# Input x loaded in quarters with its own order of the first steps, four modulation sums moved, one weight unit rounded sooner, and a smaller GpSimd share of one unit

## The chip, the cores and the metric

The kernel runs on one core of one Trainium2 chip. The metric is device time in microseconds (us) of one launch; lower is better. The times of before are the median of three runs and one profiled execution.

## The reference: what is computed

Two blocks run one after the other on x, 256 tokens of 1024 channels, all in float32. The first block has two layers (neighborhood attention and differential attention side by side), the second two layers of a modulated stack (two feed-forward parts each, a pooling mixer or an attention between them). Cut to what matters here:

```python
def first_block(x, norm_g, w_in, ..., w_out, final_g):
    for l in range(2):
        h = rmsnorm(x, norm_g[l])
        proj = h @ w_in[l]                       # 1024 -> 4096 columns: q, k, v, gate, twice
        out_a = neighborhood_attention(q_a, k_a, v_a, na_rpb[l])
        out_b = diff_attention(q_b, k_b, v_b, t5_table, lam, lam_init, subln_g[l])
        y = concat([out_a * silu(g_a), out_b * silu(g_b)])
        x = x + y @ w_out[l]
    return rmsnorm(x, final_g)

def second_block(x, c, ada_w, ada_b, norm_g, ffn_w_in, ffn_w_out, ...):
    c_silu = silu(c)
    for layer in range(2):
        mods = split(c_silu @ ada_w[layer] + ada_b[layer], 9)     # 9 vectors of 1024
        sh, sc, g = mods[0], mods[1], mods[2]
        h = rms_norm(x, norm_g[layer, 0]) * (1 + sc) + sh
        x = x + 0.5 * (1 + g) * swiglu(h, ffn_w_in[layer, 0], ffn_w_out[layer, 0])
        ...                                       # pooling mixer (layer 0) or attention (layer 1)
        ...                                       # second feed-forward part
        if layer == 0: kv = shared_kv(x, c_silu, ...)             # 2 more such vectors
    return x
```

In all, 20 modulation vectors of 1024 numbers are matrix-vector products with `silu(c)`; they depend on nothing but the inputs.

## The kernel before, in words

**Weight units.** The weights are cut into 189 units of 128 partitions x 2048 columns (1 MB). Units 0 to 15 are the input projection of the first block's layer 0, 16 to 19 its output projection, 20 to 35 and 36 to 39 those of layer 1, 40 to 61 the first feed-forward part up, 62 to 72 down, 73 the pooling weights, 74 on the second feed-forward part, and so on. Each passes through four stations. SyncE's queue (SPq) loads it into `raw`, a ring of six. ScalarE (ACT) rounds it into `w_hi`, a ring of four (`fill` on ScalarE, L641). VectorE (DVE, `lows`, L1158), GpSimd (POOL, `low`, L510) or both in halves (`shared_units`: `low_first` on GpSimd, L521, and `low_second` on VectorE, L1168) write the rest, `w_lo`, in the place of `raw`. TensorE (PE) multiplies: each float32 product is three, `w_hi` by `h_hi` (L1822), `w_hi` by `h_lo` (L1827) and `w_lo` by `h_hi` (L1835), four matmuls of 512 columns each: twelve in one "half step", which is one unit for one of the two token tiles. Two half steps use up a unit.

**Activations.** A tile of x is turned by eight transposes of 128x128 (L1914), four for the first four channel blocks ("half 0") and four for the others ("half 1"), into job banks of PSUM, of which there are three in rotation. They are then split into `h_hi` and `h_lo`. For the first projection this is `first_norm` on ScalarE and on VectorE: raw x is turned, and the norm's factor is applied when the results leave PSUM. VectorE makes `h_hi` of half 0 (L1277) and all `h_lo` (L1269), ScalarE `h_hi` of half 1 (L805). The sum of squares (L812) comes later and must be there, with its root (L1292), before ScalarE takes group 0 out of PSUM (L844).

**Order of the first steps.** `first_steps` gives (group, tile, half): (0,0,0), (0,1,0) with unit 0, (0,0,1), (0,1,1) with unit 1, then group 1 with units 2 and 3. After step 6 TensorE turns group 0's result (L1960). x comes as two loads of 512 KB: tile 0 ahead of unit 0, tile 1 behind it. Unit 0 comes in two halves. A few matmuls on zeros (`warm_up`, L2022) fill the first microseconds.

**Modulation sums.** Each vector is made in two halves. VectorE accumulates eight scaled pieces (`ada`, L1137 and L1144) into `ada_acc`; then TensorE turns this sum with four transposes (`ada_sum`, L1849), and VectorE reduces it (`reduce_vector`, L1102) and, with the second half, adds and scales (L1108, L1115). `sum_step` says after which half step of a projection layer this happens, `sum_unit` after which unit elsewhere. They follow the accumulation's end (`half_end`), pushed out of quiet stretches.

**Order.** Every engine runs its list in program order and waits on semaphores; nothing is reordered by a planner. What stands behind a waiting instruction on an engine waits too.

Of the kernel before, what the change touches and what calls it, by code (L numbers as in the profile page):

```python
# [60 lines left out]
WARM_UP = (3, 1)  # L61
SUM_STEPS = (5, 7, 9, 11, 12, 14, 15, 18, 22, 29)
# [133 lines left out]
def program(nc, known, x_in, w_in, w_out, ffn_in, ffn_out, pool_w, w_kv, w_q, w_o, ada_w, kv_ada_w,  # L196
# [60 lines left out]
    with ExitStack() as ctx:  # L257
# [78 lines left out]
        x_in_sem = [ctx.enter_context(nc.semaphore(f"x_loaded{t}")) for t in range(NT)]  # L336
# [8 lines left out]
        first_in = ctx.enter_context(nc.semaphore("first_constants_loaded"))  # L345
# [4 lines left out]
        first_consts = [(ident[:], identity), (gcols[:], norm_cols)]  # L350
# [3 lines left out]
        N_FIRST, N_CONST = 16 * len(first_consts), 16 * len(consts)  # L354
# [27 lines left out]
        assert not pool_units & shared_units  # L382

# [64 lines left out]
        def _(sp):  # L448
            sp.dma_start(x[:, 0, :], x_in[0:P, :]).then_inc(x_in_sem[0], 16)
            for u in range(NU):  # L450
# [13 lines left out]
                if u == 0:  # L464
                    sp.dma_start(x[:, 1, :], x_in[P:2 * P, :]).then_inc(x_in_sem[1], 16)
# [29 lines left out]
        def _(pool):  # L495
# [19 lines left out]
            def low_first(u):  # L515

                if u in shared_units:
                    pool.wait_ge(*S.at("w_hi_ready", u) if u else S.at("first_hi_ready"))
                    for c in range(0, UNIT // 2, LOW_PIECE):
# [111 lines left out]
        def _(act):  # L631
# [59 lines left out]
            def norm(name, last, front=norm_front):  # L691
# [5 lines left out]
                if name == "a0":  # L697
                    act.wait_ge(first_in, N_FIRST)
# [47 lines left out]
            for into, src in first_consts:  # L746
                act.dma_start(into, src).then_inc(first_in, 16)
# [41 lines left out]
            def first_norm():  # L789
# [10 lines left out]
                act.wait_ge(first_in, N_FIRST)  # L800
                for t in range(NT):
                    act.wait_ge(*S.at("xT_done", "a0", t, 1))
# [287 lines left out]
        def _(dve):  # L1090
# [72 lines left out]
            def low_second(u):  # L1163

                if u in shared_units:
                    dve.wait_ge(*S.at("w_hi_ready", u))
                    piece = slice(UNIT // 2, UNIT)
# [5 lines left out]
            def sums(upto):  # L1173

                while sums_done[0] <= min(upto, NU - 1):
                    u = sums_done[0]
                    for v, half in HALVES:
                        e = sum_unit.get((v, half), NU)
                        if e + 4 == u and up_sum(e) is None:
                            reduce_vector(v, half)  # L1180
# [79 lines left out]
            def first_norm():  # L1260
# [24 lines left out]
                lows(2)  # L1285
# [155 lines left out]
            dve.wait_ge(first_in, N_FIRST)  # L1441
            for layer in range(DEPTH):
# [154 lines left out]
            modulate_half(1, 1)  # L1597
            pooled_low_half(1, 0)
# [174 lines left out]
        def _(pe):  # L1773
# [34 lines left out]
            def half_step(u, t, nk, k_in_lhs, lhs, banks, start, stop, done=None, between=lambda: None, lo_ready=()):  # L1808
# [9 lines left out]
                for k in range(nk):  # L1818
                    if u == 0 and k == nk // 2:
                        pe.wait_ge(*S.at("w_hi_ready", 0))  # L1820
                    for c, b in enumerate(banks):
                        pe.matmul(bank(b), hi[:, k_in_lhs + k, tok], wh[:, k, c * 512:(c + 1) * 512],  # L1822
                                  start=start and k == 0, stop=False)
                lhs_wait(lo_ready)
                for k in range(nk):
                    for c, b in enumerate(banks):
                        pe.matmul(bank(b), lo[:, k_in_lhs + k, tok], wh[:, k, c * 512:(c + 1) * 512],  # L1827
                                  start=False, stop=False)
# [88 lines left out]
            def norm_T(name, t, hat=None):  # L1917
                if name == "a0":
                    pe.wait_ge(x_in_sem[t], 16)
                for half in range(2):  # L1920
                    transpose_half(name, t, half, "xT_done", [("x_hat_ready", hat or name, t)] if name != "a0" else ())
# [215 lines left out]
            pool_product(0, acc_use((("pool",), 0), ("x_ready", "f01", 0)), (0, 1, 2, 3))  # L2137
            mix_across()
# [5 lines left out]
            ada_jobs(u)  # L2144
# [201 lines left out]
```

## Time and profile before

| | |
|---|---|
| runs (3) | median 1205.9 us, 1205.85 to 1205.99 |
| profiled execution | 1205.66 us, of which span 1203.8 us |
| busy: TensorE / VectorE / ScalarE / GpSimd | 1186.5 / 799.3 / 586.5 / 559.6 us |
| share of the span | 99% / 66% / 49% / 46% |
| TensorE clock granted | full throughout |
| HBM traffic | 297.92 MB, 247 GB/s over the span |

The span is what the profiler sees between the first and the last instruction. The groups of rows further down are of the timeline: start in us from the span's start, length in us, engine, line of the kernel, operation, tile written and tiles read, shape, and how many instructions the row merges. In brackets stands the idle time of that engine just before, and what ended it. Where a row merges several instructions, its length runs from the first start to the last end.

### The profile page before, as it was taken

Reading aid. Unit: us, or ns where it says so; the run is one execution under the profiler, and the core shown is the slowest. Engines: PE = TensorE matmul, PEld = TensorE weight load, DVE = VectorE, ACT = ScalarE, POOL = GpSimd, SP = SyncE. Lnnn points to the kernel's source line nnn. Section 1 sums busy time; section 2 is a strip of 40 time slices with the busy share of each in tenths; the row PEclk is TensorE's granted clock in tenths of the full one; section 3 lists DMA queues with packets and bytes.
Section 4 is the critical chain, followed back from the end, with each engine's and each line's share of the span. In section 5 each row is a group of like instructions: output and inputs, shape, how many; then the busy total and the mean of one; then the engine's idle time right before and its main releaser. Section 6 shows DMA issues by size and latency. Waiting matters only on the chain.

```text
span 1203.8 us, 15431 instructions
## 1 busy us (share of the span) xinstructions
PE 1186.5 (99%) x5752; PEld 975.2 (81%) x5752; DVE 799.3 (66%) x1118; ACT 586.5 (49%) x764; POOL 559.6 (46%) x418
## 2 busy tenths in 40 slices
PE   8999999999999999899999999999999999999998
PEld 6888888788788888788888888888888887888887
DVE  6885468845787687678768666697673675644423
ACT  5566465665643443454434357444352665534440
POOL 1465334564454443545445226764452464445360
PEclk9999999999999999999999999999999999999999
DMA  9976369845798899459888748798884444766650
GB/s 349 356 273 234 105 237 334 280 163 172 243 342 289 293 343 352 159 164 337 296 311 312 276 175 276 248 330 299 308 295 166 150 154 157 262 215 204 210 192 35
DMA packets 183224, 297.92 MB, mean 247 GB/s; under 512 B 8368, under 2 KB 100208, under 8 KB 183152
## 3 DMA queue, kind: packets, MB, share of 16 engines
q1 hardware_dynamic: 177696, 284.82, 68.4%
q10 hardware_dynamic: 5456, 12.13, 3.0%
q8 instruction: 46, 0.75, 0.3%
q14 instruction: 26, 0.21, 0.1%
HBM read 295.84 MB, written 1.08 MB: 247 GB/s over the span
## 4 chain that ended last, share of the span: by engine, by line
PE 88%; DVE 5%; ACT 2%; POOL 2%; issue 1%; SPq 1%; DMA 1%; ACTq 0%; DVEq 0%
PE ps L1822 26%; PE ps L1835 26%; PE ps L1827 26%; PE ps L2088 2%; PE ps L1849 1%; PE ps L1972 1%; PE ps L1914 1%; PE ps L2000 1%; PE ps L1988 1%; POOL stat L501 1%; DMA raw<-w_in 1%; DVE w_lo L1158 1%; ACT w_hi L641 1%; PE ps L1960 1%; PE ps L2011 1%
## 5 line engine op out<-in xcount | busy, mean ns | idle before, releaser
L510 POOL TENSOR_TENSOR w_lo<-raw,w_hi 128x512 fp32r<-128x512 f32 x348 | 478.6, 1407 | 447.8 <-ACT w_hi L641 447.8
L641 ACT ACTIVATE w_hi<-raw 128x2048 fp32r<-128x2048 f32 x188 | 354.4, 1909 | 103.1 <-PE ps L1835 68.3
L1822 PE MATMUL ps<-w_hi,h_hi 128*128 128x512 f32 x1120 | 313.6, 402 | 1.4 <-issue 0.8
L1835 PE MATMUL ps<-w_lo,h_hi 128*128 128x512 f32 x1120 | 301.4, 391 | 1.4 <-POOL w_lo L510 0.5
L1827 PE MATMUL ps<-w_hi,h_lo 128*128 128x512 f32 x1120 | 300.5, 390 | 0.0
L1158 DVE TENSOR_TENSOR w_lo<-raw,w_hi 128x2048 fp32r<-128x2048 f32 x96 | 224.5, 2342 | 111.8 <-ACT w_hi L641 108.1
L1835 PEld LDWEIGHTS ps<-w_lo,h_hi 128*128 128x128 f32 x1120 | 209.3, 188 | 48.8 <-DVE w_lo L1158 1.7
L1827 PEld LDWEIGHTS ps<-w_hi,h_lo 128*128 128x128 f32 x1120 | 210.2, 188 | 46.0 <-DVE h_lo L1219 0.2
L1822 PEld LDWEIGHTS ps<-w_hi,h_hi 128*128 128x128 f32 x1120 | 200.6, 188 | 44.0 <-issue 6.8
L1144 DVE SCALAR_TENSOR_TENSOR ps<-ada_raw,ccol,ps 128x512 f32<-128x512 f32 x240 | 181.1, 754 | 9.1 <-DMA ada_raw<-ada_w 2.4
L914 ACT ACTIVATE a_hi<-ps 128x512 fp32r<-128x512 f32 x44 | 26.3, 599 | 160.8 <-PE ps L2088 160.8
L501 POOL TENSOR_TENSOR stat<-stat,minus_half 128x1 f32<-128x1 f32 (+3 forms) x25 | 29.1, 1166 | 151.1 <-DVE stat L1195 115.6
L1822 PE MATMUL ps<-w_hi,a_hi 128*128 128x512 f32 x348 | 95.7, 397 | 0.0
L1835 PE MATMUL ps<-w_lo,a_hi 128*128 128x512 f32 x348 | 93.8, 391 | 0.0
L1827 PE MATMUL ps<-w_hi,a_lo 128*128 128x512 f32 x348 | 93.7, 391 | 0.0
L1835 PEld LDWEIGHTS ps<-w_lo,a_hi 128*128 128x128 f32 x348 | 65.3, 188 | 14.5
L1827 PEld LDWEIGHTS ps<-w_hi,a_lo 128*128 128x128 f32 x348 | 65.4, 188 | 14.3
L1822 PEld LDWEIGHTS ps<-w_hi,a_hi 128*128 128x128 f32 x348 | 64.0, 188 | 12.9
L924 ACT ACTIVATE hn<-ps 128x512 f32<-128x512 f32 x44 | 26.3, 598 | 93.8 <-PE ps L1835 93.8
L1510 DVE SCALAR_TENSOR_TENSOR hn<-hn,ps 128x512 f32<-128x512 f32 x44 | 30.2, 686 | 58.7 <-ACT hn L924 58.6
L1503 DVE TENSOR_TENSOR a_lo<-ps,a_hi 128x512 fp32r<-128x512 f32 x44 | 30.4, 691 | 41.6 <-ACT a_hi L914 40.6
L735 ACT ACTIVATE pr<-lg,stat 128x256 f32<-128x256 f32 x64 | 31.9, 500 | 53.1 <-DVE stat L1303 53.1
(198 smaller groups left out, 979.7 us busy)
## 6 DMA issues: line engine op xcount, KB each, us to landing
raw<-ffn_in SPq DMA_DIRECT2D x176, 512.0 KB, 5.8
ada_raw<-ada_w SPq DMA_DIRECT2D x144, 512.0 KB, 7.3
raw<-ffn_out SPq DMA_DIRECT2D x44, 1024.0 KB, 6.7
raw<-w_in SPq DMA_DIRECT2D x31, 1024.0 KB, 8.5
raw<-w_out SPq DMA_DIRECT2D x8, 1024.0 KB, 6.2
ada_raw<-kv_ada_w SPq DMA_DIRECT2D x16, 512.0 KB, 9.0
raw<-w_kv SPq DMA_DIRECT2D x8, 1024.0 KB, 5.6
bias<-na_bias ACTq DMA_DIRECT2D x16, 256.0 KB, 4.3
```

Of the source, the lines that this page charges most:

```text
L501: pool.tensor_tensor(st(at, n), st(at, n), minus_half[:, 0:n], ALU.pow).then_inc(*S.inc("rsqrt_ready", *key))
L510: ins = pool.tensor_tensor(w_lo[:, u % RAW, piece], raw[:, u % RAW, piece], w_hi[:, u % RING, piece].bitcast(F32), ALU.subtract)
L641: act.activation(w_hi[:, u % RING, :], raw[:, u % RAW, :], ACT.Copy).then_inc(*S.inc("w_hi_ready", u))
L735: ins = act.activation(pr1[:, w, t, :], lg1[:, s, t, :], ACT.Exp, bias=st(rs + 2 + t), scale=-1.0, accum_out=st(rs + t))
L914: act.activation(a_hi[:, 2 * g:2 * g + 2, :].rearrange("p k c -> p (k c)"), bank(b), ACT.Copy).then_inc(*S.inc("a_hi_ready", name, g))
L1144: ins = dve.scalar_tensor_tensor(out=into, in0=src, scalar=c, in1=acc, op0=ALU.mult, op1=ALU.add)
L1158: dve.tensor_tensor(w_lo[:, u % RAW, :], raw[:, u % RAW, :], w_hi[:, u % RING, :].bitcast(F32), ALU.subtract).then_inc(*S.inc("w_lo_dve", u))
L1503: dve.tensor_tensor(a_lo[sl].rearrange("p k c -> p (k c)"), bank(b), a_hi[sl].rearrange("p k c -> p (k c)").bitcast(F32), ALU.subtract).th ...
L1510: link(dve.scalar_tensor_tensor(out=ffn_gate, in0=ffn_tanh, scalar=1.0, in1=ps[:, b:b + 2, 0:GC], op0=ALU.add, op1=ALU.mult))
L1822: pe.matmul(bank(b), hi[:, k_in_lhs + k, tok], wh[:, k, c * 512:(c + 1) * 512], start=start and k == 0, stop=False)
L1827: pe.matmul(bank(b), lo[:, k_in_lhs + k, tok], wh[:, k, c * 512:(c + 1) * 512], start=False, stop=False)
L1835: ins = pe.matmul(bank(b), hi[:, k_in_lhs + k, tok], wl[:, k, c * 512:(c + 1) * 512], start=False, stop=stop and k == nk - 1)
```

## The change

1. **x in quarters.** x comes as four loads of 256 KB (`load_x(t, half)`), the quarter (tile 0, half 0) ahead of unit 0, the other three behind it, each with a semaphore. The identity and the norm's columns have a semaphore each: the transposes wait for the identity alone.
2. **Order of the first steps.** TensorE turns one quarter before step 0, one inside step 0 and the two quarters of half 1 inside step 1, each time ahead of the `w_lo` matmuls. Steps 0 and 1 use the first half of unit 0 with both `h_hi` and `h_lo` before its second half. On ScalarE unit 1 is rounded between the two tiles' `h_hi` of half 1; `w_lo` of unit 1 stands between their `h_lo` on VectorE. `WARM_UP` goes from (3, 1) to (2, 1).
3. **Four moved sums.** In both projection layers the sum after step 29 goes to after step 31, and its reduction to behind the four `h_hi`/`h_lo` steps that follow on VectorE. Another goes from unit 43 to unit 45. The last one ahead of the pooling weights goes from unit 68 to unit 73 (`in_pool`), between the first pooling product and the mixing products of the second tile.
4. **A unit sooner.** ScalarE rounds unit `o + 4` (unit 20 in layer 0) behind the output projection's `h_hi`, ahead of the next norm's squares. In layer 1 this unit stood there already.
5. **GpSimd's share.** `shared_at`: of unit 158 GpSimd takes the first 512 columns and VectorE 1536, where each took 1024.

```diff
-WARM_UP = (3, 1)
-SUM_STEPS = (5, 7, 9, 11, 12, 14, 15, 18, 22, 29)
+WARM_UP = (2, 1)
+SUM_STEPS = (5, 7, 9, 11, 12, 14, 15, 18, 22, 31)
...
-        for a, b, wait in ((*QUIET[0], 3), (*QUIET[1], 1), (("up", 0, 0), ("up", 0, 0), 3)):
+        for a, b, wait in ((*QUIET[0], 3), (*QUIET[1], 1), (("up", 0, 0), ("up", 0, 0), 5)):
...
+    in_pool = max(h for h in sum_unit if sum_unit[h] < first["pool"])
+    sum_unit[in_pool] = first["pool"]
...
+        def shared_at(u):
+            return LOW_PIECE if u == first["up", 1, 1] + 2 else UNIT // 2
...
         @block.sync
-            sp.dma_start(x[:, 0, :], x_in[0:P, :]).then_inc(x_in_sem[0], 16)
+            def load_x(t, half):
+                cols = slice(512 * half, 512 * half + 512)
+                sp.dma_start(x[:, t, cols], x_in[t * P:(t + 1) * P, cols]).then_inc(x_in_sem[t][half], 16)
+            load_x(0, 0)
...
                 if u == 0:
-                    sp.dma_start(x[:, 1, :], x_in[P:2 * P, :]).then_inc(x_in_sem[1], 16)
+                    for t, half in ((1, 0), (0, 1), (1, 1)):
+                        load_x(t, half)
...
         first_norm() on ScalarE
-                act.wait_ge(first_in, N_FIRST)
+                act.wait_ge(gcols_in, 16)
                 for t in range(NT):
+                    if t:
+                        fill(1)
                     act.wait_ge(*S.at("xT_done", "a0", t, 1))
...
-                fill(1)
+                fill(2)
                 act.wait_ge(*S.at("stat_filled"))
                 for t in range(NT):
-                    act.wait_ge(x_in_sem[t], 16)
+                    for half in range(2):
+                        act.wait_ge(x_in_sem[t][half], 16)
                     act.activation(hn[:, t, :], x[:, t, :], ACT.Square, accum_out=st(t)).then_inc(
                         *S.inc("squares_ready", "a0", t))
-                    fill(2 + t)
-                fill(4)
+                    fill(3 + t)
...
         end of a projection layer on ScalarE, inside the loop over layers
                     high_part(("y", layer), t, 0, "yT_done")
-
-            fill(first["up", 0, 0])
+                fill(o + 4)
...
         first_norm() on VectorE
                 for t in range(NT):
                     first_low(t, 1)
-                lows(2)
+                    lows(1 + t)
...
         end of a projection layer on VectorE
                     low_part(("y", layer), t, 0, "yT_done")
+                for half in sum_step.get((layer, 31), []):
+                    reduce_vector(*half)
                 fill(o + 3)
...
             modulate_half(1, 1)
+            reduce_vector(*in_pool)
             pooled_low_half(1, 0)
...
         half_step() on TensorE
-                for k in range(nk):
-                    if u == 0 and k == nk // 2:
+                for part in (range(0, nk // 2), range(nk // 2, nk)) if u == 0 else (range(nk),):
+                    if u == 0 and part[0]:
                         pe.wait_ge(*S.at("w_hi_ready", 0))
...              (w_hi by h_hi, then lhs_wait(lo_ready), then w_hi by h_lo, for the k of each part)
                 def between(s):
                     if s == 0 and not layer:
-                        norm_T(name, 1)
+                        raw_T(1, 0)
+                    if s == 1 and not layer:
+                        raw_T(0, 1)
+                        raw_T(1, 1)
...
             pool_product(0, acc_use((("pool",), 0), ("x_ready", "f01", 0)), (0, 1, 2, 3))
+            ada_jobs(u)
             mix_across()
```

What stands in a row on TensorE at the start of the program, before (`ps<-ident,x` are the transposes of x, `ps<-row` the matmuls on zeros):

```order
L2022 MATMUL ps<-row 128x512 x3
L1914 MATMUL ps<-ident,x 128x128 x8
L2022 MATMUL ps<-row 128x512
L1822 MATMUL ps<-w_hi,h_hi 128x512 x4
L1827 MATMUL ps<-w_hi,h_lo 128x512 x4
L1914 MATMUL ps<-ident,x 128x128 x8
L1835 MATMUL ps<-w_lo,h_hi 128x512 x4
L1822 MATMUL ps<-w_hi,h_hi 128x512 x4
L1827 MATMUL ps<-w_hi,h_lo 128x512 x4
L1835 MATMUL ps<-w_lo,h_hi 128x512 x4
```

And now, from the second transposes on (lines 1839, 1844, 1852 and 1931 are 1822, 1827, 1835 and 1914 of before):

```order
L1839 MATMUL ps<-w_hi,h_hi 128x512 x2
L1844 MATMUL ps<-w_hi,h_lo 128x512 x2
L1931 MATMUL ps<-ident,x 128x128 x4
L1852 MATMUL ps<-w_lo,h_hi 128x512 x4
L1839 MATMUL ps<-w_hi,h_hi 128x512 x2
L1844 MATMUL ps<-w_hi,h_lo 128x512 x2
L1839 MATMUL ps<-w_hi,h_hi 128x512 x2
L1844 MATMUL ps<-w_hi,h_lo 128x512 x2
L1931 MATMUL ps<-ident,x 128x128 x8
L1852 MATMUL ps<-w_lo,h_hi 128x512 x4
```

All sixteen transposes stood ahead of the first `w_lo` matmuls; now eight of them, those of half 1, stand behind step 1's `w_hi` matmuls.

ScalarE from the first rounding on, before (`w_hi<-raw` of 1024 columns is a half of unit 0, of 2048 columns units 1, 2, 3 and 4 in turn; `hn,stat<-x` are the squares of one tile):

```order
L797 ACTIVATE w_hi<-raw 128x1024
L805 ACTIVATE h_hi<-ps,gcols 128x128 x8
L641 ACTIVATE w_hi<-raw 128x2048
L812 ACTIVATE hn,stat<-x 128x1024
L641 ACTIVATE w_hi<-raw 128x2048
L812 ACTIVATE hn,stat<-x 128x1024
L641 ACTIVATE w_hi<-raw 128x2048 x2
```

And now:

```order
L808 ACTIVATE w_hi<-raw 128x1024
L818 ACTIVATE h_hi<-ps,gcols 128x128 x4
L652 ACTIVATE w_hi<-raw 128x2048
L818 ACTIVATE h_hi<-ps,gcols 128x128 x4
L652 ACTIVATE w_hi<-raw 128x2048
L826 ACTIVATE hn,stat<-x 128x1024
L652 ACTIVATE w_hi<-raw 128x2048
L826 ACTIVATE hn,stat<-x 128x1024
L652 ACTIVATE w_hi<-raw 128x2048
```

The rounding of unit 1 stands behind `h_hi` of (tile 0, half 1), which waits for the moved transposes; unit 2 now stands ahead of the first squares, unit 3 between them.

VectorE at the end of layer 0's projection, before (`mods<-` is the reduced sum, `w_lo<-raw,w_hi` x2 are units 18 and 19):

```order
L1219 TENSOR_TENSOR yn_lo<-ps,yn_hi 128x4x128
L1102 TENSOR_REDUCE mods<-ps 128x4
L1108 TENSOR_TENSOR mods<-mods,bcols 128x8
L1115 SCALAR_TENSOR_TENSOR mods<-mods,gcols 128x8
L1458 SCALAR_TENSOR_TENSOR ga<-ga,ps 128x1024
...
L1207 TENSOR_TENSOR ps<-ps,subc 128x512
L1219 TENSOR_TENSOR h_lo<-ps,h_hi 128x4x128
L1158 TENSOR_TENSOR w_lo<-raw,w_hi 128x2048 x2
```

And now:

```order
L1232 TENSOR_TENSOR yn_lo<-ps,yn_hi 128x4x128
L1471 SCALAR_TENSOR_TENSOR ga<-ga,ps 128x1024
...
L1220 TENSOR_TENSOR ps<-ps,subc 128x512
L1232 TENSOR_TENSOR h_lo<-ps,h_hi 128x4x128
L1115 TENSOR_REDUCE mods<-ps 128x4
L1121 TENSOR_TENSOR mods<-mods,bcols 128x8
L1128 SCALAR_TENSOR_TENSOR mods<-mods,gcols 128x8
L1171 TENSOR_TENSOR w_lo<-raw,w_hi 128x2048 x2
```

The three operations of the sum stand directly ahead of `w_lo` of unit 18. In layer 1 it is the reduction alone, ahead of unit 38.

## Rows read from the trace of the kernel before

**Rows 1.** The page, part 1: busy time of TensorE, share, instructions.
```profile
PE 1186.5 (99%) x5752; PEld 975.2 (81%) x5752; DVE 799.3 (66%) x1118; ACT 586.5 (49%) x764; POOL 559.6 (46%) x418
```

**Rows 2.** Timeline of the first 31 us, the instructions that set the start.
```profile
6.65 1.09 PE L1914 MATMUL ps<-ident,x 128*128 128x128 f32 x8 [0.85 <-DMA gcols<-norm_cols]
7.11 1.06 ACT L794 ACTIVATE w_hi<-raw 128x1024 fp32r<-128x1024 f32 x1 [3.95 <-DMA raw<-w_in]
...
8.32 3.61 POOL L521 TENSOR_TENSOR w_lo<-raw,w_hi 128x512 fp32r<-128x512 f32 x2 [7.48 <-ACT w_hi L794]
8.47 1.06 ACT L797 ACTIVATE w_hi<-raw 128x1024 fp32r<-128x1024 f32 x1 [0.30 <-DMA raw<-w_in]
...
9.56 1.23 DVE L1168 TENSOR_TENSOR w_lo<-raw,w_hi 128x1024 fp32r<-128x1024 f32 x1 [0.29 <-ACT w_hi L797]
...
11.98 1.20 PE L1835 MATMUL ps<-w_lo,h_hi 128*128 128x512 f32 x4
12.15 1.14 ACT L805 ACTIVATE h_hi<-ps,gcols 128x128 fp32r<-128x128 f32 x4 [1.59 <-PE ps L1914]
...
13.16 1.93 ACT L641 ACTIVATE w_hi<-raw 128x2048 fp32r<-128x2048 f32 x1
...
14.97 1.07 ACT L812 ACTIVATE hn<-x 128x1024 f32<-128x1024 f32 x1
...
15.75 1.07 PE L1822 MATMUL ps<-w_hi,h_hi 128*128 128x512 f32 x4
...
22.39 1.92 ACT L641 ACTIVATE w_hi<-raw 128x2048 fp32r<-128x2048 f32 x1 [1.61 <-DMA raw<-w_in]
...
26.55 0.16 DVE L1292 TENSOR_SCALAR stat<-stat 128x2 f32<-128x2 f32 x1
...
28.70 1.26 ACT L844 ACTIVATE hn<-ps,stat 128x512 f32<-128x512 f32 x2 [0.72 <-issue]
...
30.02 1.09 PE L1960 MATMUL ps<-ident,hn 128*128 128x128 f32 x8
```

**Rows 3.** Timeline of the ends of both projection layers.
```profile
121.75 0.60 PE L1849 MATMUL ps<-ident,ada_acc 128*128 128x128 f32 x4
...
124.35 0.68 DVE L1102 TENSOR_REDUCE mods<-ps 128x4 f32<-128x512 f32 x1
...
125.26 0.17 DVE L1115 SCALAR_TENSOR_TENSOR mods<-mods,gcols 128x8 f32<-128x8 f32 x1
...
131.49 1.16 PE L1822 MATMUL ps<-w_hi,yn_hi 128*128 128x512 f32 x4 [0.56 <-DVE ga L1458]
...
140.67 4.48 DVE L1158 TENSOR_TENSOR w_lo<-raw,w_hi 128x2048 fp32r<-128x2048 f32 x2
...
143.10 1.11 PE L1835 MATMUL ps<-w_lo,h_hi 128*128 128x512 f32 x4
...
278.21 1.16 PE L1822 MATMUL ps<-w_hi,yn_hi 128*128 128x512 f32 x4 [0.24 <-DVE ga L1458]
```

**Rows 4.** Timeline where layer 1's projection begins (unit 20).
```profile
153.26 5.05 POOL L510 TENSOR_TENSOR w_lo<-raw,w_hi 128x512 fp32r<-128x512 f32 x4 [3.06 <-ACT w_hi L641]
...
158.37 1.19 PE L1835 MATMUL ps<-w_lo,h_hi 128*128 128x512 f32 x4 [0.54 <-POOL w_lo L510]
```

**Rows 5.** Timeline, the sum after unit 43.
```profile
328.94 0.66 PE L1849 MATMUL ps<-ident,ada_acc 128*128 128x128 f32 x4 [0.72 <-DVE ada_acc L1144]
```

**Rows 6.** Timeline of the pooling mixer, second tile.
```profile
507.29 1.13 PE L1927 MATMUL ps<-bands,hn 128*128 128x128 f32 x8 [2.27 <-DVE hn L1570]
...
509.98 0.69 DVE L1581 TENSOR_TENSOR h_lo<-ps,h_hi 128x512 fp32r<-128x512 f32 x1 [1.38 <-ACT h_hi L955]
```

**Rows 7.** Timeline where the last feed-forward part begins (units 157 and 158).
```profile
1015.80 1.67 DVE L1168 TENSOR_TENSOR w_lo<-raw,w_hi 128x1024 fp32r<-128x1024 f32 x1
...
1018.67 1.20 PE L1835 MATMUL ps<-w_lo,h_hi 128*128 128x512 f32 x4 [0.47 <-POOL w_lo L521]
...
1020.37 1.09 PE L1914 MATMUL ps<-ident,hn 128*128 128x128 f32 x8 [0.51 <-ACT hn L654]
```

More of the change, by code:

```diff
@@ L335, in program @@
         bias_in = [ctx.enter_context(nc.semaphore(f"bias_in{i}")) for i in range(BIASES)]
-        x_in_sem = [ctx.enter_context(nc.semaphore(f"x_loaded{t}")) for t in range(NT)]
+        x_in_sem = [[ctx.enter_context(nc.semaphore(f"x_loaded{t}_{half}")) for half in range(2)] for t in range(NT)]
         ROWS = {("down", 0, 0): 2, "pool": 5, "pool_scale": 4, "pool_shift": 3, ("down", 0, 1): 8,
@@ L344, in program @@
         half_in = ctx.enter_context(nc.semaphore("first_half_loaded"))
-        first_in = ctx.enter_context(nc.semaphore("first_constants_loaded"))
+        ident_in = ctx.enter_context(nc.semaphore("identity_loaded"))
+        gcols_in = ctx.enter_context(nc.semaphore("norm_columns_loaded"))
         const_in = ctx.enter_context(nc.semaphore("constants_loaded"))
@@ L349, in program @@
         out_sem = ctx.enter_context(nc.semaphore("out_stored"))
-        first_consts = [(ident[:], identity), (gcols[:], norm_cols)]
         consts = [(bcols[:], ada_b_cols),
@@ L518, in low_first @@
                     pool.wait_ge(*S.at("w_hi_ready", u) if u else S.at("first_hi_ready"))
-                    for c in range(0, UNIT // 2, LOW_PIECE):
+                    for c in range(0, shared_at(u), LOW_PIECE):
                         piece = slice(c, c + LOW_PIECE)
@@ L744, in load_bias @@
                     bias_in[i % BIASES], 16)
-            for into, src in first_consts:
-                act.dma_start(into, src).then_inc(first_in, 16)
+            act.dma_start(ident[:], identity).then_inc(ident_in, 16)
+            act.dma_start(gcols[:], norm_cols).then_inc(gcols_in, 16)
             act.wait_ge(*S.at("minus_half_ready"))
@@ L1166, in low_second @@
                     dve.wait_ge(*S.at("w_hi_ready", u))
-                    piece = slice(UNIT // 2, UNIT)
+                    piece = slice(shared_at(u), UNIT)
                     dve.tensor_tensor(w_lo[:, u % RAW, piece], raw[:, u % RAW, piece],
@@ L1178, in sums @@
                         e = sum_unit.get((v, half), NU)
-                        if e + 4 == u and up_sum(e) is None:
+                        if e + 4 == u and up_sum(e) is None and e != first["pool"]:
                             reduce_vector(v, half)
@@ L1440, in _ @@
             dve.memset(stat[:], 1.0).then_inc(*S.inc("stat_filled"))
-            dve.wait_ge(first_in, N_FIRST)
+            dve.wait_ge(gcols_in, 16)
             for layer in range(DEPTH):
@@ L1817, in half_step @@
                     return
-                for k in range(nk):
-                    if u == 0 and k == nk // 2:
+                for part in (range(0, nk // 2), range(nk // 2, nk)) if u == 0 else (range(nk),):
+                    if u == 0 and part[0]:
                         pe.wait_ge(*S.at("w_hi_ready", 0))
[L1821 to L1828, printed above, removed]
+                    for k in part:
+                        for c, b in enumerate(banks):
+                            pe.matmul(bank(b), hi[:, k_in_lhs + k, tok], wh[:, k, c * 512:(c + 1) * 512],
+                                      start=start and k == 0, stop=False)
+                    lhs_wait(lo_ready)
+                    for k in part:
+                        for c, b in enumerate(banks):
+                            pe.matmul(bank(b), lo[:, k_in_lhs + k, tok], wh[:, k, c * 512:(c + 1) * 512],
+                                      start=False, stop=False)
                 between()
@@ L1917, in norm_T, with raw_T @@
             def norm_T(name, t, hat=None):
-                if name == "a0":
-                    pe.wait_ge(x_in_sem[t], 16)
                 for half in range(2):
-                    transpose_half(name, t, half, "xT_done", [("x_hat_ready", hat or name, t)] if name != "a0" else ())
+                    transpose_half(name, t, half, "xT_done", [("x_hat_ready", hat or name, t)])
+            def raw_T(t, half):
+                pe.wait_ge(x_in_sem[t][half], 16)
+                transpose_half("a0", t, half, "xT_done")
             def mix_part(half, to, of):
@@ L2025, in _ @@
             warm_up(WARM_UP[0])
-            pe.wait_ge(first_in, N_FIRST)
+            pe.wait_ge(ident_in, 16)
             for layer in range(DEPTH):
@@ L2029, in _ @@
                 if layer == 0:
-                    norm_T(name, 0)
+                    raw_T(0, 0)
                     warm_up(WARM_UP[1])
@@ L2143, in _ @@
             S.same("unit_used", (u,), "acc_done", (("pool",), NT - 1))
-            ada_jobs(u)
             ffn(0, 1, "f01", 8, "kv")
```

4 lines of the change are left out of this document (2 added, 2 removed).

## Prediction

> **What bounds the kernel now.** I read the page first: TensorE is busy for 1186.5 us of a span of 1203.8 us [rows 1]. So this kernel can only win what is left of TensorE's idle time, some 17 us, and it loses whatever makes TensorE wait more. Then I listed TensorE's own rows of the timeline that carry a bracket, since each is a wait that the other engines did not cover, and looked at the two or three engines around each: the start, the ends of the two projection layers, the first units after a norm, the pooling mixer. Each edit sits at one of these places. Between them TensorE runs without a gap, so a delay at one place moves all behind it and is not made good; every engine hangs from TensorE's step ends there. The sum is therefore a sum of shifts.
>
> **The start: what it removes.** TensorE waits for the norm's columns at 6.65 before its first transposes [rows 2]; now it waits for the identity alone. That gives nothing by itself: the next matmuls wait for ScalarE's rounding of the first half of unit 0. This half was there at 7.11 and the second at 8.47, so 512 KB take 1.36 us of the queue. With a quarter of x less ahead (256 KB) both come 0.68 us sooner, at about 6.43 and 7.79; at worst, no sooner. GpSimd's two pieces of `w_lo`, 3.61 us long, followed the first rounding at once and TensorE's first `w_lo` matmuls came at 11.98, right at the end of these pieces (8.32 + 3.61 = 11.93) [rows 2]. Now: rounding done 7.5, pieces done 11.3, `w_lo` matmuls at 11.3. The gain here is 0.68 us. The third warm-up matmul and the finer order of steps 0 and 1 lie inside this wait and cost nothing. The two more load commands delay the commands behind them; the cover is unit 4, which came at 22.39 with ScalarE waiting for it [rows 2], and which ScalarE reaches now only at 24.8 (below).
>
> **The start: what it adds.** A half step without waits takes at most (30.02 - 15.75)/5 = 2.85 us, and 2.73 when the waits in it are taken off; four matmuls are a third, 0.91. After 11.3: four `w_lo` matmuls 0.91, step 1's eight `w_hi` matmuls 1.82, four transposes of the quarter (0,1) 0.55 (the four of [rows 3] at 121.75 take 0.60 with their tail). ScalarE gets them at 14.6. It has been idle since 8.9, because what is queued next is `h_hi` of this quarter, and the rounding of unit 1 is queued behind that. So `h_hi` 1.14, to 15.8; rounding of unit 1 1.93, to 17.7 [durations, rows 2]. Step 2 needs both and starts at 17.8, where it started at 15.75 before: 2.05 us later. Before, unit 1 was rounded at 13.16 to 15.09, since the transposes stood ahead of the first `w_lo` matmuls.
>
> The loss grows behind it. ScalarE goes on: `h_hi` of (1,1) 1.14, unit 2 1.93, squares 1.04, unit 3 1.93, squares 1.04: 17.7 + 7.1 = 24.8. VectorE waits for the second squares before it takes `w_lo` of units 3 and 4 (2.24 us each, 4.48 for two [rows 3]), and only then makes the root's half (L1292): 25.0 + 4.6 = 29.7, where it was 26.55. ScalarE's evacuation of group 0 followed 2.15 us behind (28.70) and TensorE's L1960 3.47 us behind (30.02) [rows 2]. So L1960 comes at 33.2, 3.2 us late. TensorE itself would be there at 17.8 + 5 x 2.73 + 0.5 (a wait for `w_lo` of unit 1, which VectorE has at 17.8 + 2.3 = 20.1 against 19.6) = 31.9; it waits 1.3. From there on everybody is shifted alike. **Start: +3.2 us**, and 2.4 to 4.3 if each of these steps is a little shorter, or if the halves come no sooner.
>
> **The ends of the projection layers.** The four transposes of the sum (an `L1849` row; 0.44 us of TensorE's stream, from 121.75 to the next matmuls without their tail) leave the stream before the wait for the gate and go into it. This wait is 0.56 us in layer 0 and 0.24 us in layer 1 [rows 3]; in layer 1 what is over moves the next chain, which hangs from the same step end. I take -0.44 each, 0 to -0.56. But the reduction now stands directly ahead of `w_lo` of unit 18 on VectorE. That ran 140.67 to 142.96, and TensorE's `w_lo` matmuls began at 143.10: no slack, beyond 0.1. In layer 0 the three operations took 124.35 to 125.43, 1.08 us, so TensorE stalls 1.0; in layer 1 it is the reduction alone, 0.68, and the same pattern, so 0.65. Bounds: 0 (if VectorE got to it earlier) to 1.1 and 0.7. Both ends together: -0.9 + 1.65 = **+0.75**.
>
> **Unit 20 sooner.** GpSimd's four pieces began at 153.26 after waiting 3.06 us for ScalarE, which had the norm's squares and scaling ahead of the rounding, and TensorE waited 0.54 for them [rows 4]. ScalarE has the time for the rounding while it waits for x. **-0.54**, 0 at the other end.
>
> **Unit 43 to 45.** The wait of 0.72 for VectorE's accumulation goes [rows 5]; two units later the sum is long done. **-0.72**.
>
> **Unit 68 to 73.** The transposes leave a full stretch and go ahead of the mixing products, where TensorE waits 2.27 us for VectorE [rows 6]. The whole chain that ends this wait begins at a step end behind unit 68, so it comes 0.44 sooner: **-0.44**. The reduction (0.68) is put on VectorE ahead of `h_lo` at 509.98, ahead of which it idled 1.38 waiting for ScalarE [rows 6]; that covers it. Without this cover it would cost up to 0.68.
>
> **Unit 158.** TensorE waited 0.47 for GpSimd's pieces and then 0.51 for the scaled x [rows 7]. VectorE's part grows from 1024 to 1536 columns: 1.23 us alone [rows 2] becomes 1.8, and here 1024 took 1.67, so about 2.2, from 1015.80 to 1018.0. The first wait goes, but the mean for the norm's root is queued behind this operation, so the second wait grows by most of it: **-0.2**, between -0.47 and +0.1.
>
> The Trainium skill bears on this place: "SBUF — State Buffer", section "Who interferes with whom", says that a VectorE operation with two SBUF inputs and a GpSimd one that reads SBUF exclude each other for the whole instruction, whoever is first. The trace agrees in that 1.67 against 1.23 is a delay, not a rate; by the rule VectorE's operation would end at 1018.1, and the sum would be the same.
>
> **Sum.** +3.2 + 0.75 - 0.54 - 0.72 - 0.44 - 0.2 = +2.05 us. The profiled execution took 1205.66 us; the changed one 1207.7. The median of the runs is 0.24 above the profiled one: **1208.0 us**. About 0.2% (2.4 us: 1203.5 to 1208.3) is what a measurement of this kernel can tell from no change, so this is just inside.
>
> **Rivals.**
> - *The start gives its 0.68 us and takes nothing back.* This needs ScalarE to have `h_hi` of (0,1) and unit 1 rounded by 15.1, as before. For it: the start's edits all shorten the first wait. Against it: ScalarE's list, in which unit 1 stands behind the moved transposes. Sum -0.68 + 0.75 - 1.9 = -1.8, 1204.1; with the stalls of unit 18 and 38 hidden as well, -3.5, 1202.4.
> - *Slower: the halves of unit 0 come no sooner.* Place: the first rounding at 7.11. The three loads share the engines, so a smaller load ahead need not bring those behind it forward. Price: the 0.68 comes back on the whole chain, as all of it hangs from GpSimd's pieces: +2.7, 1208.6. It decides from a first rounding later than about 6.8: then the sum passes 2.4.
> - *The port.* GpSimd's second piece and VectorE's half of unit 0 become ready together, at about 8.9. Before, VectorE's 1.23 us came first (its operation at 9.56 kept its length, while GpSimd's pair took 3.61 us). If GpSimd's piece is first, the `w_lo` matmuls are no later, but VectorE's `h_hi` of (1,0) is, and with it step 1: 0.4 to 0.7 later, 1208.5. The rule of the Trainium skill named above (section "Who interferes with whom") allows this order, since by it whoever starts first keeps the port.
>
> **How the numbers follow.** Forecast 0.45, start without loss 0.2, halves no sooner 0.22, the port 0.13. The forecast's own range is 1206.3 to 1209.6: start 2.4 to 4.3, the encoder's stalls half to full, the other gains each 70 to 100%. The range to hold 8 in 10 reaches on to the first rival: 1204.0 to 1209.9. Faster: half of the first rival and a rest of unknown slack, 0.13. Slower: most of the second and third and the upper third of the forecast, 0.4. Same: 0.47.
>
> **What would show it.** Right: ScalarE idle for 5 us or more between the second half of unit 0 and `h_hi` of (0,1); the third group of `w_hi` matmuls (step 2) at 17 to 18.5 with TensorE waiting for ScalarE; a wait of about 1 us before the first `ps<-ident,hn` transposes, at about 33; waits of 1.0 and 0.65 us for `w_lo` of units 18 and 38; no wait at unit 20, none for `ada_acc` after unit 45; the wait in the mixer 0.4 to 0.5 shorter. Wrong: a step 2 that starts before 16.5, or `w_lo` of unit 18 in time although the sum stands ahead of it.

## The result, and the profile after

The changed kernel takes 1207.2 us by median (20 runs, 1206.1 to 1209.3), the kernel before 1205.9 in the same comparison (20 runs, 1205.0 to 1206.5). The ratio is 1.0013, with a 95% interval of 1.0007 to 1.0018: slower by 0.8 to 2.2 us, which is inside the 0.2% named in the prediction. The forecast was 1208.0. Ten of the 20 runs of after had a mean granted TensorE clock of 1.000 and a median of 1206.7; the ten others, with 0.997 to 0.999, took 1207.2 to 1209.3.

The profiled execution of after took 1206.67 us, its span 1204.7. The page's first part answers to [rows 1]: TensorE is busy for 0.9 us more, VectorE for 2.9 us more. Of this, 1.4 us is its halves of the units shared with GpSimd (9.2 for 7.8): its larger share of unit 158, and a wait for GpSimd inside its operation for unit 0 (below). The rest is spread over small operations.

```profile
PE 1187.4 (99%) x5750; PEld 976.4 (81%) x5750; DVE 802.2 (67%) x1118; ACT 585.9 (49%) x764; POOL 560.6 (47%) x417
```

Timeline of the start of after, against [rows 2]. Columns as there: start and length in us, engine, line, what is written and read, and in brackets the idle time before it with what ended it.

```profile
5.50 1.06 ACT L805 ACTIVATE w_hi<-raw 128x1024 fp32r<-128x1024 f32 x1 [2.33 <-DMA raw<-w_in]
...
6.70 2.52 POOL L532 TENSOR_TENSOR w_lo<-raw,w_hi 128x512 fp32r<-128x512 f32 x2 [5.86 <-ACT w_hi L805]
...
8.20 2.12 DVE L1181 TENSOR_TENSOR w_lo<-raw,w_hi 128x1024 fp32r<-128x1024 f32 x1
...
10.46 1.17 PE L1852 MATMUL ps<-w_lo,h_hi 128*128 128x512 f32 x4 [0.26 <-DVE w_lo L1181]
...
14.34 1.14 ACT L818 ACTIVATE h_hi<-ps,gcols 128x128 fp32r<-128x128 f32 x4 [6.18 <-PE ps L1931]
15.35 1.93 ACT L652 ACTIVATE w_hi<-raw 128x2048 fp32r<-128x2048 f32 x1
...
17.42 1.16 PE L1839 MATMUL ps<-w_hi,h_hi 128*128 128x512 f32 x4 [1.83 <-ACT w_hi L652]
...
32.06 1.09 PE L1979 MATMUL ps<-ident,hn 128*128 128x128 f32 x8 [0.28 <-ACT hn L857]
```

The first `w_lo` matmuls come 1.52 us sooner than before (10.46 against 11.98). Then ScalarE stands idle for 6.18 us, with unit 1's rounding queued behind the transposes of the quarter (0,1). TensorE waits 1.83 us for that rounding, and the transposes of the turned result come at 32.06, 2.04 us later than in [rows 2].

Behind the start, rows of after against [rows 3 to 7]:

```profile
142.38 0.68 DVE L1115 TENSOR_REDUCE mods<-ps 128x4 f32<-128x512 f32 x1
...
143.50 4.49 DVE L1171 TENSOR_TENSOR w_lo<-raw,w_hi 128x2048 fp32r<-128x2048 f32 x2
...
145.84 1.20 PE L1852 MATMUL ps<-w_lo,h_hi 128*128 128x512 f32 x4 [0.88 <-DVE w_lo L1171]
...
163.87 4.50 DVE L1171 TENSOR_TENSOR w_lo<-raw,w_hi 128x2048 fp32r<-128x2048 f32 x2 [0.67 <-POOL stat L512]
...
166.22 1.21 PE L1852 MATMUL ps<-w_lo,h_hi 128*128 128x512 f32 x4
...
292.47 1.19 PE L1852 MATMUL ps<-w_lo,h_hi 128*128 128x512 f32 x4 [0.35 <-DVE w_lo L1171]
...
508.60 1.13 PE L1946 MATMUL ps<-bands,hn 128*128 128x128 f32 x8 [1.84 <-DVE hn L1585]
...
1017.10 2.21 DVE L1181 TENSOR_TENSOR w_lo<-raw,w_hi 128x1536 fp32r<-128x1536 f32 x1
```

The waits at the gates (131.49 and 278.21 before), at unit 20 (158.37), behind unit 43 (328.94) and for GpSimd at unit 158 (1018.67) are gone. New are 0.88 and 0.35 us for `w_lo` behind the moved sums: VectorE begins with the reduction at 142.38 and comes to `w_lo` only at 143.50. The mixer's wait is 1.84 instead of 2.27. One more place is new, with no bracket because the idle time is short: at 166.22, behind unit 20, `w_lo` comes 0.4 us late for TensorE (told below with the sum).

### The profile page after: what moved, and what is told of

It reads as the page before. It is cut to its first block, busy times and chain, and to the rows that moved or that the text cites. A ratio compares the mean times of both kernels' runs of the same rounds, so it can differ in the third digit from the quotient of the medians.

```text
span 1204.7 us, 15430 instructions
## 1 busy us (share of the span) xinstructions
PE 1187.4 (99%) x5750; PEld 976.4 (81%) x5750; DVE 802.2 (67%) x1118; ACT 585.9 (49%) x764; POOL 560.6 (47%) x417
## 4 chain that ended last, share of the span: by engine, by line
PE 88%; DVE 6%; ACT 3%; issue 2%; POOL 1%; DMA 0%; SPq 0%; ACTq 0%; DVEq 0%
PE ps L1839 26%; PE ps L1852 26%; PE ps L1844 26%; PE ps L2110 2%; PE ps L1931 1%; PE ps L1991 1%; PE ps L1866 1%; DVE w_lo L1171 1%; PE ps L2019 1%; PE ps L2007 1%; ACT w_hi L652 1%; POOL stat L512 1%; PE ps L1979 1%; PE ps L2030 1%; ACT h_hi L672 1%
## 5 line engine op out<-in xcount | busy, mean ns | idle before, releaser
L1518 DVE TENSOR_TENSOR a_lo<-ps,a_hi 128x512 fp32r<-128x512 f32 x44 | 30.4, 692 | 40.7 <-ACT a_hi L927 39.7
```

The lines of the kernel that those rows point to most:

```text
L1518: dve.tensor_tensor(a_lo[sl].rearrange("p k c -> p (k c)"), bank(b), a_hi[sl].rearrange("p k c -> p (k c)").bitcast(F32), ALU.subtract).th ...
```

## The experiments

Ratios are to the kernel before, timed in the same comparison. Experiments 1 to 4, 5 to 8, and 9 and 10 are three such comparisons; the kernel before had 1205.6, 1205.9 and 1205.6 us in them, and the changed kernel was in none, so its 1207.2 is that of the result.

**1. The start alone** (the kernel before with the start's edits: quarters, order, semaphores, `WARM_UP = (2, 1)`).

> The kernel before with the start's edits alone (x in quarters, the order of the first steps, two warm-up matmuls ahead); sums, unit 20 and unit 158 as before. Theory (the start costs, the rest gives back): in the changed kernel the first transposes of the turned result stood at 32.06 against 30.02, so 2.0 us later than before, 1207.9 us by median, and more where the clock rises late. Rival (the start is free, the rest costs): within 0.3 of before, 1206.0.

1208.9 us (6 runs), ratio 1.0028 (1.0016 to 1.0039): 3.3 us slower. The start costs more than the whole change, and the theory held in sign; the size is larger than the 2.0 that the trace of after shows. Why is told below, with the landings.

**2. The rest alone** (before's start; sums, unit 20, unit 158 as changed).

> The changed kernel's moved sums, unit 20 and unit 158 with the start of before. Theory: the shifts behind the start in the changed kernel's trace go from +2.04 to +0.90, so this is 1.1 us faster than before, 1204.8 by median, with stalls of 0.9 and 0.35 us for w_lo of units 18 and 38, and with a spread of runs as narrow as before (1.6 us). Rival (the rest costs, by my sum's terms with the stalls at 1.0 and 0.65 and the gains not there): 1206.5.

1203.7 us, ratio 0.9984 (0.9975 to 0.9993): 1.9 us faster, range 1203.4 to 1204.3. The two parts add up: +3.3 - 1.9 = +1.4, and the change as a whole measured +1.3. The waits of 0.88 and 0.35 us stand in this trace too, at 142.68 (the row below) and 289.31:

```profile
142.68 1.20 PE L1844 MATMUL ps<-w_lo,h_hi 128*128 128x512 f32 x4 [0.88 <-DVE w_lo L1164]
```

**3. The third warm-up matmul back.**

```diff
-WARM_UP = (2, 1)
+WARM_UP = (3, 1)
```

> The changed kernel with the third warm-up matmul back. Theory A (the clock): the third matmul fills TensorE until the identity comes; with it the engine gets its full clock at about 4.5 us as before, and the runs of 1207.3 to 1209.3 with a mean granted clock below 1 go: median 1206.6, spread under 1.5 us. Theory B (my prediction: the third matmul lies in a wait and costs nothing): same times as the changed kernel, 1207.2, with the same spread of 3 us.

1208.5 us, ratio 1.0025 (1.0015 to 1.0035): 1.2 us slower than the changed kernel. Both theories fell; full clock came at 7.49 us in this trace, not at 4.5 as the first had it. TensorE's rows of this kernel:

```profile
1.45 5.49 PE L2041 MATMUL ps<-row 128*128 128x512 f32 x6 [1.45 <-DVE row L1452]
6.73 0.98 PE L1931 MATMUL ps<-ident,x 128*128 128x128 f32 x4
7.54 1.02 PE L2041 MATMUL ps<-row 128*128 128x512 f32 x2
8.57 0.74 PE L1839 MATMUL ps<-w_hi,h_hi 128*128 128x512 f32 x2
```

The transposes wait for nothing but the warm-up, which runs to 6.73; in after they stood at 5.03. The first `w_hi` matmuls come at 8.57 instead of 6.95, the first `w_lo` matmuls at 11.57 instead of 10.46. The turned result comes at 33.68, so between these two traces the third matmul costs 1.6 to 1.7 us.

**4. Unit 1 ahead of `h_hi` of (0,1) on ScalarE.**

```diff
+                fill(1)
                 for t in range(NT):
-                    if t:
-                        fill(1)
```

> The changed kernel with one line of ScalarE's list moved: unit 1 is rounded ahead of h_hi of (0,1) instead of behind it. Theory (ScalarE's list sets the start): step 2 begins at 15.6 to 16.2 instead of 17.42, the first transposes of the turned result at 30.4 to 30.8 instead of 32.06, and the time falls by 1.2 to 1.6 us. Rival (unit 1 itself comes late, or the squares chain sets 32.06 by itself): step 2 after 17, time as the changed kernel.

1206.2 us, ratio 1.0005 (0.9996 to 1.0014): 1.0 us less than the changed kernel, where 1.2 to 1.6 were expected. The rows:

```profile
12.52 1.92 ACT L652 ACTIVATE w_hi<-raw 128x2048 fp32r<-128x2048 f32 x1 [3.69 <-DMA raw<-w_in]
...
14.59 2.17 ACT L817 ACTIVATE h_hi<-ps,gcols 128x128 fp32r<-128x128 f32 x8
...
15.76 1.13 DVE L1281 SCALAR_TENSOR_TENSOR h_lo<-ps,gcols,h_hi 128x128 fp32r<-128x128 f32 x4 [3.35 <-ACT h_hi L817]
15.78 1.19 PE L1838 MATMUL ps<-w_hi,h_hi 128*128 128x512 f32 x4
...
16.80 2.28 DVE L1170 TENSOR_TENSOR w_lo<-raw,w_hi 128x2048 fp32r<-128x2048 f32 x1
...
19.14 1.20 PE L1851 MATMUL ps<-w_lo,h_hi 128*128 128x512 f32 x4 [1.00 <-DVE w_lo L1170]
```

Step 2 begins at 15.78 without a wait, as expected. But 1.00 us of the gain is lost at 19.14, where TensorE waits for `w_lo` of unit 1: VectorE has `h_lo` of (0,1), which still hangs from the late transposes, ahead of it. The turned result comes at 31.07, where 30.4 to 30.8 was expected.

**5. The transposes of (0,1) ahead of the first `w_lo` matmuls.**

```diff
                     if s == 0 and not layer:
                         raw_T(1, 0)
+                        raw_T(0, 1)
                     if s == 1 and not layer:
-                        raw_T(0, 1)
                         raw_T(1, 1)
```

> The changed kernel with the transposes of the quarter (0,1) ahead of the first w_lo matmuls instead of behind step 1's w_lo wait. Theory (the place of these transposes in TensorE's order holds up ScalarE): h_hi of (0,1) at about 11 instead of 14.34, unit 1 rounded when it lands (12.5), step 2 at about 16 without a wait, the first transposes of the turned result at 29.8 to 30.5 instead of 32.06, time 1.6 to 2.2 us less, 1205.3. Rival (only ScalarE's order matters): no better than unit 1 first, 31.1 and 1206.2.

1205.3 us, ratio 0.9995 (0.9987 to 1.0004): 1.9 us less than the changed kernel. The rows:

```profile
9.51 1.03 PE L1931 MATMUL ps<-ident,x 128*128 128x128 f32 x8
...
10.64 1.15 ACT L818 ACTIVATE h_hi<-ps,gcols 128x128 fp32r<-128x128 f32 x4 [2.22 <-PE ps L1931]
...
12.28 1.92 ACT L652 ACTIVATE w_hi<-raw 128x2048 fp32r<-128x2048 f32 x1 [0.49 <-DMA raw<-w_in]
...
14.92 1.08 PE L1839 MATMUL ps<-w_hi,h_hi 128*128 128x512 f32 x4
...
29.86 1.09 PE L1979 MATMUL ps<-ident,hn 128*128 128x128 f32 x8 [1.15 <-ACT hn L857]
```

ScalarE has `h_hi` of (0,1) at 10.64 and rounds unit 1 at 12.28, when it lands; step 2 begins at 14.92 without a wait, and the turned result comes at 29.86, now behind a wait of 1.15 us for ScalarE. So the place of these four transposes in TensorE's order causes 1.9 of the start's 3.3 us; ScalarE's list is how it gets to the other engines. The full clock came early in this trace (4.47 us, 6.92 in after), but that isn't what made the difference: in experiment 10, which has these transposes in the same place, it came at 6.29, and step 2 began at 15.01.

**6. The sums of step 31 reduced behind the output projection's `w_lo`.**

```diff
-                for half in sum_step.get((layer, 31), []):
-                    reduce_vector(*half)
                 fill(o + 3)
+                for half in sum_step.get((layer, 31), []):
+                    reduce_vector(*half)
```

> The changed kernel with the reduction of the step-31 sums moved on VectorE from ahead of w_lo of units 18 to 19 (38 to 39) to behind it. Theory (the reduction is what makes TensorE wait): the waits of 0.88 and 0.35 us for w_lo at 145.84 and 292.47 go, the hole before the output projection stays closed, and the time falls by 1.2 to 1.5 us, to about 1205.9. Rival (ScalarE's rounding of the unit is late anyway, since it too runs into the layer's end): the waits stay above 0.5 in sum and the time falls by less than 0.5.

1205.8 us, ratio 0.9998 (0.9989 to 1.0007): 1.4 us less than the changed kernel. VectorE and TensorE there:

```profile
142.40 4.48 DVE L1171 TENSOR_TENSOR w_lo<-raw,w_hi 128x2048 fp32r<-128x2048 f32 x2
...
144.83 1.11 PE L1852 MATMUL ps<-w_lo,h_hi 128*128 128x512 f32 x4
...
146.80 0.69 DVE L1115 TENSOR_REDUCE mods<-ps 128x4 f32<-128x512 f32 x1
...
148.77 1.23 DVE L1269 TENSOR_TENSOR x<-ps,x 128x1024 f32<-128x1024 f32 x1 [0.88 <-PE ps L1852]
```

`w_lo` begins at 142.40 instead of 143.50 and TensorE doesn't wait. The reduction now lies in VectorE's idle time ahead of the update of x, of which 0.88 us is still left.

**7. The same with the start of before** (experiments 2 and 6 together).

> The start of before, all other edits of the change, and the reduction of the step-31 sums behind w_lo of units 18/19 and 38/39. If the three effects add: 1203.7 - 1.2 = 1202.5 us, 3 us faster than before. Rival (the parts overlap: what is gained at the layer's end is lost in the next norm, whose transposes need a bank or whose x update needs VectorE): 1203.5.

1202.6 us, ratio 0.9972 (0.9962 to 0.9983). The effects add; this is 3.3 us faster than before and, across comparisons, 4.7 faster than the changed kernel.

**8. Two warm-up matmuls in the kernel before.**

```diff
-WARM_UP = (3, 1)
+WARM_UP = (2, 1)
```

> The kernel before with two warm-up matmuls ahead of the transposes instead of three. Theory (in the start of before the transposes wait for the norm's columns, so the third warm-up matmul costs nothing there; it costs 1.2 us only where the transposes wait for the identity alone): no change, within 0.4 us of before, transposes still after 5.8. Rival (it costs in any start): 1 us faster. Third possibility (it is needed for the clock): full clock later and 0.5 us or more slower.

1207.0 us, ratio 1.0009 (1.0000 to 1.0018): some 1.1 us slower (0 to 2.2), where I expected no change. The start doesn't show it (the turned result comes at 29.12). The profiled execution has a stretch at the lower clock right behind the mixer's wait. By stretch: from and to, us, busy time of TensorE, its weight loads, VectorE, ScalarE and GpSimd, then the granted clock:

```profile
505.00:507.00 2.00, 0.53 (x5) 0.56 (x6) 1.97 (x4) 1.12 (x2) 0.53 (x1) 1.00 0.00 1
507.00:508.00 1.00, 0.81 (x7) 0.58 (x6) 0.74 (x2) 0.51 (x1) 1.00 (x2) 0.72 0.00 0
508.00:510.00 2.00, 2.00 (x10) 2.00 (x11) 0.69 (x1) 1.18 (x3) 2.00 (x2) 0.50 0.00 0
```

Up to the mixer TensorE is 0.9 us ahead of the trace of before, and behind this stretch 0.1 us late: it cost 1.0 us in this execution. All 11 of its runs had a mean granted clock below 1.000. But so had 27 of the 29 runs of before in this comparison, and those took 1205.9 and not 1207. What makes this kernel slower stays open.

**9. Experiments 5 and 6 together.**

> The changed kernel with both mends: the transposes of the quarter (0,1) ahead of the first w_lo matmuls, and the step-31 reductions behind the output projection's w_lo. If they add (1.9 and 1.4 us off the changed kernel's 1207.2): 1204.0. Its start still ends in a wait of 1.15 us of TensorE for ScalarE's evacuation of group 0 (at 29.86), so it stays 1.4 us behind the start of before with the same mended sums, 1202.6.

1203.2 us, ratio 0.9981 (0.9972 to 0.9990): a little better than the sum. The wait for ScalarE ahead of the turned result is there, 0.86 us in this trace, the slowest of the 11 runs: the second half of unit 0 was rounded only at 9.09.

**10. The same, with VectorE's `w_lo` of unit 4 behind the root's half and the small constants.**

```diff
-                lows(4)
+                lows(3)
                 dve.wait_ge(*S.at("rsqrt_ready", "a0"))
                 dve.tensor_scalar(st(2, NT), st(0, NT), 0.5, ...).then_inc(*S.inc("half_root_ready"))
...
                     constants()
+                    lows(4)
```

> The kernel of the run e_T_early_late with VectorE's w_lo of unit 4 moved behind the norm's root half and the small constants. Theory (my prediction's step: VectorE takes w_lo of units 3 and 4 ahead of what the evacuation waits for, and this sets the first transposes of the turned result): ScalarE's evacuation goes ahead at 26.5 instead of 28.54, the wait of 1.15 us goes, 28.7 instead of 29.86, time 1202.9. Rival (w_lo of unit 4 then comes late, or the constants wait for their loads): the wait moves to another place and the time stays at 1204.0.

1202.6 us, ratio 0.9975 (0.9966 to 0.9984), 0.6 less than experiment 9, where 1.1 was expected. The small constants and the evacuation come at once:

```profile
24.17 0.17 DVE L1305 TENSOR_SCALAR stat<-stat 128x2 f32<-128x2 f32 x1 [0.60 <-POOL stat L512]
24.25 0.61 DVE L1325 TENSOR_TENSOR lamr<-lamr 128x128 f32<-128x128 f32 x2
...
26.33 1.27 ACT L857 ACTIVATE hn<-ps,stat 128x512 f32<-128x512 f32 x2 [0.72 <-PE ps L1853]
...
27.30 2.29 DVE L1171 TENSOR_TENSOR w_lo<-raw,w_hi 128x2048 fp32r<-128x2048 f32 x1
...
28.67 1.03 PE L1980 MATMUL ps<-ident,hn 128*128 128x128 f32 x8
```

The theory held in its mechanism: the wait is gone, and `w_lo` of unit 4 is in time at 27.30. The gain is half of what was expected. This kernel (new start, mended twice) and that of experiment 7 (old start) both beat the kernel before, by 3.0 and 3.3 us: mended, the new start draws level with the old one and is no gain over it. No run has x in quarters with the old order of steps, so what the four loads do by themselves isn't shown.

## Why the prediction was right, step by step

The forecast was 0.8 us above the measured median, and +2.05 us on the profiled time where the profiled executions differ by 1.0. Between these two traces all of this gap lies in the start, +2.04 for +3.2. By the runs of experiments 1 and 2 it lies in the rest: -1.9 for -1.15, and the start is +3.3. That the start's size fits the runs so well is partly luck: my end point, 33.2, was 1.1 us too late, and the 30.02 that I counted from was 0.9 us later than in three other traces of the old start.

*Start, predicted +3.2.* In the two profiled executions it is 30.02 to 32.06, +2.04; alone, by runs, it is +3.3. The difference is mostly what the profile of before happened to show. In it the first half of unit 0 was rounded at 7.11 [rows 2]. In the traces of three more kernels with this start it was 6.05, 6.04 and 6.18, and the turned result came at 29.00, 29.18 and 29.12: the execution that I had read was 1 us late there. The eight traces with x in quarters have 5.19 to 5.67. So 256 KB less ahead is worth 0.67 us (mean 5.42 against 6.09), where I took 0.68; against the one trace that I had it looks like 1.61. And with the new order the turned result goes from 29.1 to 32.06, 3.0 us later.

*How the loss comes about.* The mechanism was as told: ScalarE idle for over 5 us (6.18), step 2 at 17.4 (predicted 17.8), waiting for the rounding of unit 1. What sets the first `w_lo` matmuls was wrong. I had them at 11.3, at the end of GpSimd's pieces; these ended at 9.22, and the matmuls came at 10.46, waiting 0.26 us for VectorE's half. The last link was too long. I had the turned result at 33.2 with a wait of 1.3 us, and it came at 32.06 with 0.28: step 2 was 0.4 us ahead of my sum, ScalarE's list from there to the second squares took 0.4 less, and VectorE 0.3 less. VectorE took `w_lo` of units 3 and 4 from 24.18 to 28.67, where I had 25.0 to 29.6. This order of VectorE is a bound once the transposes are earlier: taking it away in experiment 10 gave 0.6 us.

*The third warm-up matmul "cost nothing".* This step was wrong. It held while the halves of unit 0 came last; but they landed before TensorE had `h_hi` (6.95, behind the transposes at 5.03). Experiment 3 shows the price of the third matmul there: 1.2 us. The removed one is a gain that my sum doesn't have: with three, the first `w_lo` matmuls came at 11.57, with two at 10.46, and I had 11.3.

*The rest, predicted -1.15.* By shifts of the same instruction between the two traces: gate of layer 0 -0.34 (predicted -0.44); `w_lo` of unit 18 +1.04 (+1.0); unit 20 and the gate of layer 1 together -0.75 (-0.98); `w_lo` of unit 38 +0.52 (+0.65); the sums of units 43 and 68 together -1.20 (-1.16); unit 158 -0.41 (-0.2). The sum is -1.14. The -0.75 hides a loss that my sum doesn't have. Unit 20 itself gave 0.8 and the gate of layer 1 gave 0.4, but between them the shift grows by 0.4 at 166.22: ScalarE's squares and VectorE's mean came as late as if unit 20 had gained nothing (the squares at 161.88 against 159.05 before, +2.83, while TensorE had come down to +2.0), and `w_lo`, begun at 163.87, was no longer in time. At unit 158 VectorE's operation took the predicted 2.21 us, but the second wait grew only from 0.51 to 0.66. The root on GpSimd waits for the mean, as I had it. In the kernel before, though, it also stood behind GpSimd's own second piece and began only at 1018.58, 1.05 us behind the mean; with one piece less it follows the mean (1019.23) at 1019.45. My sum left out that the removed piece was ahead of the root. The runs put the rest at -1.9, with an interval from -3.0 to -0.8 that holds both. Of the 0.75 us between, the clock may be some 0.2: 19 of 25 runs of before had a mean granted clock below 1.000, against 2 of 11 here, and such runs of before took 0.3 us more. It may be more than that, which is argued and not shown: the profiled execution of before was late at the start but had no stretch at the lower clock, while behind the mixer's wait such a stretch cost 0.6 to 1.0 us in three other traces (last section). The two may stand in for each other in the runs of before.

*The rivals.* The start that takes nothing back (1204.1) fell with ScalarE's 6.18 us. That the halves come no sooner is half true: the first did (0.67 us), the second was rounded at 6.92 to 9.09 with the new start and at 7.41, 7.54 and 7.52 in the three traces with the old one. But the first `w_lo` matmuls came at 10.30 to 10.62 where two warm-up matmuls stood ahead and the second half was there in time, and at 11.0 in those three, so the price that the rival named, 0.68 us on the whole chain, wasn't paid there. In the one execution where the second half came at 9.09, `w_lo` came at 12.04. The port came about: in the trace of after GpSimd's pieces went first and took 2.52 us, VectorE's half 2.12; in [rows 2] they took 3.61 and 1.23. But it cost next to nothing. TensorE's `w_lo` matmuls waited 0.26 for VectorE and came at 10.46; in the trace of experiment 1, where VectorE's half again took 1.23, they came at 10.36.

## What to carry to other kernels

When a step of TensorE's order is moved, look at what is queued behind it on the engine that takes its result: a rounding that had nothing to do with these transposes stood behind them, and moving four transposes by one half step was worth 1.9 us. A wait that is closed by moving work into it is a gain only if the other half of the work, here the reduction, doesn't land ahead of a value with no slack; one place further on it was free. And where a single profiled execution shows a load's landing, other traces of the same start may differ by 1 us; a term that hangs from it needs that much range.

## What the runs showed of the hardware

**Half clock behind a wait.** In the trace of experiment 1, TensorE waited 1.82 us ahead of step 2, at 17.83, worked for 0.8 us, and then was granted half its clock, the 1.2 GHz level, for about 3.4 us. By stretch, as above; the clock is the number behind the five engines:

```profile
17.00:18.00 1.00, 0.17 (x1) 0.20 (x2) 0.33 (x2) 1.00 (x3) 0.00 (x0) 1.00 1.10 324
18.00:19.00 1.00, 1.00 (x5) 0.79 (x5) 1.00 (x1) 1.00 (x4) 0.00 (x0) 0.82 1.06 389
19.00:22.00 3.00, 3.00 (x9) 2.33 (x8) 3.00 (x6) 3.00 (x4) 0.00 (x0) 0.50 1.06 395
22.00:24.00 2.00, 2.00 (x10) 1.68 (x9) 1.25 (x1) 2.00 (x2) 0.00 (x0) 0.99 1.05 387
```

After has the same wait (1.83) and no such stretch in its profiled execution. From step 2 to the turned result it took 14.64 us at the full clock, experiment 1 took 15.30: 0.66 us for the stretch. Behind the mixer's wait it came in three of the profiled executions (experiments 4, 6 and 8, behind 1.84, 1.83 and 2.28 us) and not in the others, whose waits there were as long (1.84 in after, 2.27 before). By TensorE's shift against the trace of after (4, 6) or before (8) it cost 0.6, 0.8 and 1.0 us. So a wait of 2 us may cost more than its length, and not in every execution.

**When the full clock comes.** TensorE's first matmul began at 1.45 us in every trace, at the 1.2 GHz level. Full clock was granted from 4.52 us in the profiled execution of before (which the table of the kernel before calls full throughout), from 5.85 and 5.52 in experiments 2 and 7 with the same start, from 6.92 in after, and from 4.47 to 7.66 in the others; the three warm-up matmuls of experiment 3 didn't bring it sooner (7.49).

**Two engines on one port.** In after VectorE's half began at 8.20 and ended at 10.32, that is 1.10 us behind the end of GpSimd's second piece (6.70 + 2.52 = 9.22). In experiment 2 it ended at 10.88, 1.09 behind 9.79. Alone it takes 1.23 [rows 2], so it waited and then ran at its own pace; it wasn't slowed. The small operation for the root on GpSimd shows the same from the other side: 2.68 us in experiment 10, begun 0.18 us behind a `w_lo` operation of VectorE, where the kernel before needed 0.71. The rows of experiment 10:

```profile
21.28 2.29 DVE L1171 TENSOR_TENSOR w_lo<-raw,w_hi 128x2048 fp32r<-128x2048 f32 x1
21.46 2.68 POOL L512 TENSOR_TENSOR stat<-stat,minus_half 128x2 f32<-128x2 f32 x1 [12.22 <-DVE stat L1301]
```

And in the kernel before:

```profile
20.42 0.71 POOL L501 TENSOR_TENSOR stat<-stat,minus_half 128x2 f32<-128x2 f32 x1 [8.49 <-DVE stat L1288]
```

This agrees with the Trainium skill, "SBUF — State Buffer", section "Who interferes with whom", by which the two exclude each other for the whole instruction, whoever is first; the order of GpSimd's and VectorE's halves did change between executions of the same start.
